# Group 0's first two z products moved into the prologue, and the v pair's seventh product between the two v transposes

## The reference, cut to what matters

```
p = u @ w_in                                # q, k, v, z and the gates
qkv = silu(centred_dwconv(p[:4096], 5 taps))
q, k = l2_norm(q), l2_norm(k)
t_inv = (I + A)^-1 of each 64 row chunk     # A from k, the decays and beta
scan over chunks in both directions         # state, v_new, o
y = (rms_norm(o_f + o_b) * silu(z)) @ w_out
```

## Time and profile before

| | before |
|---|---|
| median of 3 runs | 2900.93 us (2897.48 to 2902.15) |
| the profiled execution | 2898.26 us |
| its span in the trace | 2896.3 us |
| mean granted TensorE clock | 0.984 of full speed |
| PE (TensorE) busy | 2749.9 us, 95% |
| DVE (VectorE) busy | 1495.1 us, 52% |
| ACT (ScalarE) busy | 942.6 us, 33% |
| POOL (GpSimd) busy | 364.2 us, 13% |
| PE's share of the chain that ended last | 85% |

### The profile page before, as it was taken

How to read it: one execution, slowest core, us unless ns; L and a number is a source line. 1 busy time by engine, 2 the same in 40 slices (tenths; PEclk the granted TensorE clock), 3 DMA queues, 4 the chain that set the end, 5 groups by cost and what they waited for, 6 DMA issues and landing times.

```text
span 2896.3 us, 38659 instructions
## 1 busy us (share of the span) xinstructions
PE 2749.9 (95%) x15874; PEld 1896.7 (65%) x15874; DVE 1495.1 (52%) x2932; ACT 942.6 (33%) x2245; POOL 364.2 (13%) x268
## 2 busy tenths in 40 slices
PE   8799999999999989999999989999999999999998
PEld 3567667676776757654644335588677664688886
DVE  3466676767767645632343334433357321777732
ACT  1426355463654632012333223322224311222200
POOL 0221110111111000000000022113113220000031
PEclk9899999999999999999999999999999999999999
DMA  5110111101111152321000002021132111221220
GB/s 226 45 40 21 62 23 45 52 21 47 28 55 52 46 177 110 124 87 66 30 29 22 34 20 102 30 88 59 73 117 88 44 73 66 109 87 59 97 93 29
DMA packets 77263, 193.60 MB, mean 67 GB/s; under 512 B 56000, under 2 KB 60224, under 8 KB 65568
## 3 DMA queue, kind: packets, MB, share of 16 engines
q1 hardware_dynamic: 54656, 186.65, 17.8%
q10 hardware_dynamic: 22432, 4.49, 0.8%
HBM read 181.16 MB, written 9.96 MB: 66 GB/s over the span
## 4 chain that ended last, share of the span: by engine, by line
PE 85%; DVE 8%; ACT 4%; issue 1%; DMA 1%; ACTq 0%; SPq 0%; DVEq 0%
PE ps L1364 11%; PE ps L1828 10%; PE ps L2028 9%; PE ps L1278 8%; PE ps L1575 6%; PE ps L2056 4%; PE ps L1845 3%; PE ps L1968 3%; PE ps L1706 2%; DVE arena L2860 2%; PE ps L1434 2%; PE ps L1456 2%; PE ps L1444 2%; PE ps L1718 1%; PE ps L1405 1%; ACT arena L2086 1%
## 5 line engine op out<-in xcount | busy, mean ns | idle before, releaser
L2085 ACT ACTIVATE arena<-ps 64x128 f32<-64x128 f32 (+8 forms) x723 | 287.4, 414 | 826.8 <-PE ps L1364 217.7
L1364 PE MATMUL ps<-arena 128*128 128x385 f32 x1232 | 425.5, 497 | 5.1 <-ACT arena L2085 5.1
L1364 PEld LDWEIGHTS ps<-arena 128*128 128x128 f32 x1232 | 231.8, 193 | 156.0 <-issue 13.8
L1828 PE MATMUL ps<-arena 128*128 128x256 f32 x1456 | 328.6, 380 | 2.0 <-ACT arena L2085 2.0
L1828 PEld LDWEIGHTS ps<-arena 128*128 128x128 f32 x1456 | 271.7, 191 | 40.3 <-issue 5.9
L2028 PE MATMUL ps<-arena 128*128 128x256 f32 x1176 | 254.6, 378 | 0.0
L2028 PEld LDWEIGHTS ps<-arena 128*128 128x128 f32 x1176 | 222.4, 189 | 32.5 <-issue 0.5
L1278 PE MATMUL ps<-arena 128*128 128x512 f32 x496 | 220.7, 604 | 14.7 <-DVE arena L3123 5.1
L1278 PEld LDWEIGHTS ps<-arena 128*128 128x128 f32 x496 | 95.3, 193 | 138.4 <-issue 130.0
L2086 ACT ACTIVATE arena<-ps,arena 128x128 f32<-128x128 f32 x544 | 156.4, 379 | 75.4 <-PE ps L1509 46.1
L1575 PE MATMUL ps<-arena 128*128 128x512 f32 (+1 forms) x512 | 170.3, 488 | 0.3 <-DVE arena L2952 0.3
(11 more groups left out here) (360 smaller groups left out, 4277.0 us busy)
## 6 DMA issues: line engine op xcount, KB each, us to landing
arena<-in_ada_w SPq DMA_DIRECT2D x12, 2048.0 KB, 8.9
arena<-in_w_up SPq DMA_DIRECT2D x11, 2048.0 KB, 8.0
arena<-in_w_dil SPq DMA_DIRECT2D x9, 2048.0 KB, 7.8
arena<-in_w_dn SPq DMA_DIRECT2D x8, 2048.0 KB, 8.7
arena<-in_w_gate SPq DMA_DIRECT2D x6, 2048.0 KB, 7.6
arena<-in_w_down SPq DMA_DIRECT2D x4, 2816.0 KB, 9.5
arena<-in_att_in SPq DMA_DIRECT2D x5, 2048.0 KB, 7.9
arena<-in_w_z SPq DMA_DIRECT2D x8, 1024.0 KB, 4.9
```

The source lines that it names most:

```text
L1364: m = e.matmul(ps[:, bank, 0:HALF_PAD], left[:, k], right[:, k], start=first and k == 0, stop=k == 3, skip_group_check=not first)
L1828: m = e.matmul(ps[:, bank, 0:256], left[:, k], right[:, k], start=first and k == 0, stop=k == 3, skip_group_check=not first)
L2085: return e.activation(out, x, ACT.Copy)
```

## The change

Three edits go together.

1. P1 and P2 of group 0's z pair leave the lists behind the first joins and are placed in four halves in the prologue: the first half of P1 behind `decay` of chunk 3, its second half and the first half of P2 behind `gram` of chunk 3, the second half of P2 behind `decay` of chunk 5. VectorE's addition of P2 is placed behind `conv(0, 3)`.
2. The z pair of group 0 gets banks 4 (a), 0 (b), and 5 for P2 and 1 for P3 (c). Before it had 0, 1 and 4.
3. In groups 0 to 6, P7 of the next v pair is placed between `turn(j, 0)` and `turn(j, 1)`. Before it stood behind both.

```diff
@@ prologue
+    z = unit(0, 2, "P1") + unit(0, 2, "P2")
     yield from (("exp", 0, 0), ("exp", 0, 1), ("gram", 0, 0), ("gram", 0, 1), *scaled(0, 0), p[14], *scaled(0, 1))
     yield from (*grams(4, 2), *conv(0, 2), p[15])
-    yield from (("exp", 0, 4), ("exp", 0, 2), ("gram", 0, 4), ("gram", 0, 2), *grams(3), *scaled(0, 4))
-    yield from (("exp", 0, 3), *scaled(0, 2), ("gram", 0, 3), *scaled(0, 3), *grams(5), ("exp", 0, 5))
-    yield from (("gram", 0, 5), *scaled(0, 5), *unit(1, 0, "P1"), *conv(0, 3))
+    yield from (("exp", 0, 4), ("exp", 0, 2), ("gram", 0, 4), ("gram", 0, 2), *grams(3), *z[:1], *scaled(0, 4))
+    yield from (("exp", 0, 3), *scaled(0, 2), ("gram", 0, 3), *z[1:3], *scaled(0, 3), *grams(5), ("exp", 0, 5))
+    yield from (*z[3:], ("gram", 0, 5), *scaled(0, 5), *unit(1, 0, "P1"), *conv(0, 3), ("pair_add", 0, 2, "P2"))
@@ group
             yield "turn", j, 0
+            yield from unit(k, 1, "P7")
             yield "turn", j, 1
             t = [x for n in range(4) for x in conv(k, n)]
             yield from t[:2]
-            yield from unit(k, 1, "P7")
             yield "pair_add", k, 1, "P7"
@@
+            if j == 0:
+                behind = [[x for x in more if x not in z and x != ("pair_add", 0, 2, "P2")] for more in behind]
@@ banks
-        def pair_banks(j, p):
+        def pair_banks(j, p, name):
+            if (j, p) == (0, 2):
+                return 4, 0, 5 if name == "P2" else 1
             return (0, 1, 7) if (j, p) == (7, 2) else PAIR_BANKS[p]
```

More of the change, by code:

```diff
@@ L1343, in pair_product @@
             def pair_product(j, p, name, part):
-                (a, b, c), (a_, b_) = pair_banks(j, p), pair_weights(j, p)
+                (a, b, c), (a_, b_) = pair_banks(j, p, name), pair_weights(j, p)
                 s = [quarter(S_dn, n) for n in range(4)]
@@ L2192, in pair_snap @@
                     e.wait_ge(*at("y", j - 1))
-                copy(pair_half(j, p, place_), ps[:, pair_banks(j, p)[0], 0:HALF_PAD]).then_inc(*mark(f"pair_{event}", j, p))
+                copy(pair_half(j, p, place_), ps[:, pair_banks(j, p, name)[0], 0:HALF_PAD]).then_inc(*mark(f"pair_{event}", j, p))
             def silu(j, *tiles):
@@ L2777, in pair_add @@
             def pair_add(j, p, name):
-                _, b, c = pair_banks(j, p)
+                _, b, c = pair_banks(j, p, name)
                 place_, bank, old, new = {"P2": (11, c, "snap1", "c11"), "P5": (12, b, "snap2", "u4"),
```

## The result

| | before | changed |
|---|---|---|
| median | 2899.20 us of 4 runs (2896.47 to 2902.15) | 2875.93 us of 4 runs (2871.40 to 2882.39) |
| span of the profiled execution | 2896.3 us | 2869.0 us |
| mean granted TensorE clock there | 0.984 | 0.989 |

The ratio is 0.9923, with a 95% interval of 0.9909 to 0.9936; of 2899.20 us that is 22.3 us less (18.6 to 26.4; the two medians lie 23.3 apart). The forecast was 20.8 us less and 2880.1 us.

The account below looks back on a forecast made before the run. PE, busy 95% of the span, was taken as the bound, its largest wait at the second `turn`. -14.4 - 3.4 - 5.6 + 2.6 + 0 = -20.8 us, from 2900.9 to 2880.1 us; range 2873 to 2890.

Parts of the forecast that it names:

- The turns: Groups 0 to 6: P7 between the turns covers PE's whole wait for VectorE's copy of the first turn; -14.4 us.
- the returning blocks: Rival: late `back` transfers set the first join, PE waits there for what the turns saved; 2897.9 us, chance 0.04.
- The clock: From second turn to first join: without PE's pause the falls in groups 1 and 4 go; -3.4 us, bounds 0 and 3.4.
- The joins of group 0: Behind group 0's joins PE is rid of P1, P2 and a shared slot without new waiting; -5.6 us, bounds 0 and -5.6.
- The prologue: Four halves between chunk steps, taken as 0 (bounds -0.3 and +5.2), plus a new wait for bank 5, +2.6 us.
- Its new wait: P2 of pair (1, 0) waits for bank 5 until VectorE's addition behind `conv(0, 3)`; P6 one product later, +2.6 us.
- The halves between the chunk steps: Prologue: four halves of P1 and P2, paid for by the clock rising by about 135 to 138; taken as 0.
- the rivals: Clock falls elsewhere 0.12, prologue at half clock 0.08, copy-bound joins 0.04, returning blocks 0.04, slower with VectorE the bound 0.03.
- The first of them: Falls of the clock turn up at other pauses of PE in each group; -17.4, 2883.5 us, chance 0.12.

Follow-up runs that it names:

- the three profiles with the wait: Traces of the kernel before, executed twice, and of the changed kernel with P7 put back behind both turns (ratio 0.9981 to the kernel before).
- the middle load: Kernel with the late load, its 2 MB load held only to the end of the second join step's first group; 12.05 us from first to fourth step.
- half P7: Changed kernel with only the first half of P7 between the turns, the second half behind both; ratio 0.9947 to the kernel before.
- two kernels: Changed kernel with z's P2 in bank 6 (0.9911), or with its addition ahead of `conv(0, 3)` (0.9909); ratios to the kernel before.
- the late load: Kernel with the addition ahead of `conv(0, 3)`, with group 2's 2 MB weight load held to the end of the third join step; 0.9910 to the kernel before.

## Why the prediction was right

**The turns, -14.4 forecast, -16.0 measured.** PE's wait was all gain, as argued: P7 was ready, VectorE had the time, the returning blocks had landed. The term was too small because I took the idle time in the row as the whole price of a wait. Six groups gave 2.36 and group 0 gave 1.8, each 0.2 more than its idle row. Half a product gave the same surcharge. So the term that was mis-sized is this one, 14.4 for 16.0.

**The clock, -3.4 forecast.** In the profiled pair it was -3.4: two falls before, none after. Over the three profiles with the wait a fall came in 5 of 21 stretches, 1.7 per execution, so on average the term is nearer 1.7 x 1.68 = 2.8. The forecast was read from one profile, and that its two falls lie near the average is luck. The Trainium skill (TensorE: Matmul & The Clock Gate, HAM oscillation), weighed in the prediction, warns of long idle gaps; that a short one leaves the clock alone is what the prediction inferred from it, and the traces do not agree, since a wait of about 2.1 us was followed by the lower level in 5 cases of 18.

**The joins of group 0, -5.6 forecast, -5.15 measured.** No copy was waited for, as argued from VectorE's idle time (the 4.54 us of the earlier trace rows lie ahead of VectorE's first piece in the second step, not between the second and third, which changes nothing). What I had not seen is that the z products also kept the small matmuls apart: without them TensorE comes to the next block of its code before the block is there. Without the pause the joins give 5.8. The changed kernel had the smallest of the seven pauses (0.7 us of the stretch; with the middle load or half P7 it was 2.0 to 2.5, clock included), so a near hit of this term in the profile is in part luck too.

**The prologue.** Its new wait was forecast at +2.6 and measured at +2.2, shown to be the bank by two kernels. The halves between the chunk steps cost 0, as forecast. The clock rose as argued, and sooner: it was up by the end of the first half of P1 (131.4), where the forecast had 135 to 138. These are the windows of the changed kernel that answer to the earlier trace rows:

```profile
132.00:136.00 4.00, 3.55 (x16) 2.13 (x16) 3.93 (x5) 2.79 (x9) 4.00 (x3) 1.00 0.00 0
...
144.00:148.00 4.00, 0.00 (x0) 0.00 (x0) 3.89 (x5) 0.18 (x1) 0.00 (x0) 0.56 0.26 54
148.00:152.00 4.00, 3.77 (x7) 2.23 (x8) 0.17 (x1) 0.31 (x1) 0.00 (x0) 0.59 0.03 11
152.00:156.00 4.00, 4.00 (x14) 2.30 (x13) 0.56 (x1) 0.49 (x1) 0.00 (x0) 1.00 0.00 0
```

Two things make 2.2 out of 2.6. The pause ended sooner: P2 starts 20.73 us behind `decay` of chunk 3, where P6 started 20.94 behind it before, because P2 waits for VectorE's addition and P6 for ScalarE's copy. And the clock was low while PE stood idle ahead of 148.23, so 3.0 us of the working time behind the pause fell on the lower level instead of 3.4, which is worth another 0.2 us.

So the sum of -20.8 against -22.3 is 1.6 too little for the turns, 0.45 too much for the joins and 0.4 too dear for the bank, with the clock as in the profiled pair. None of the rivals happened in the changed kernel. The first of them (the falls turn up at other pauses) did happen in a small way in three of the kernels made from it, behind the pause in the joins. The forecast of 2880.1 started from a median of 2900.93; the median beside which the change was timed is 2899.20. The fastest kernel by the timed runs is the changed one with its addition moved ahead of the convolution (0.9909), with the late load beside it at 0.9910; both intervals overlap that of the change.

## What to carry to other kernels

A wait of TensorE costs more than the idle time in its row: some 0.2 us of draining and refilling, and at times a fall of the clock behind it, so work that is ready belongs in it even where it fills only a part. When a product moves to another bank, ask who releases that bank and what stands ahead of the release in that engine's queue; here one line of order was worth 2.2 us. And work that stands between runs of very small matmuls gives their code time to arrive: see which large load starts beside such a run before taking it out.

## What the runs showed of the hardware that I had not expected

- Pauses of 0.6 to 1.5 us within 288 records of small matmuls in a row (one each 30 ns), in seven of seven kernels with a 2 MB load beside them and in neither of the two executions with the load held back. TensorE goes on 1.3 to 1.5 us after a 16 KB block of its code has landed.
- After all three of the pauses of 1.15 us or more the clock fell as well (a fourth join step of 3.52, 3.88 and 4.29 us instead of 3.02, and the half product ahead of it 2.66, 2.27 and 1.81 instead of 1.56), so such a pause can cost up to 1.6 us again.
- A first tap of VectorE's convolution took 1.82 or 1.36 us beside a memset of GpSimd, 0.62 otherwise, and ended 0.41 us behind the memset in both orders.
- The clock of a whole execution differs between runs of one kernel (0.984 to 0.989 in the changed one, 2882.39 to 2871.40 us); a difference of a few us can be told only from stretches of the trace between the same two steps.
